# Output stage of a hybrid decoder on one core: the 32 sample rows projected in four column groups beside the first prompt tile, instead of as a ninth tile

## What is computed

```
hn  = (h - mean(h)) * rsqrt(var(h) + EPS)            # per head, 4 heads of 512
out = (hn * gamma + skip * ca) * silu(z)             # 2048 columns
y   = rmsnorm(h_residual + out @ w_out, final_norm_g)   # w_out: 2048 x 1024
```

## Time and profile before

| | us |
|---|---|
| median of 3 runs | 2202.44 |
| lowest and highest | 2199.47, 2211.96 |
| the profiled execution | 2200.57 |
| its span in the profile | 2198.9 |
| mean granted TensorE clock in it | 0.951 of full speed |

### The profile page before, as it was taken

One profiled execution on the slowest core, in us unless ns is written; L12 is line 12 of the kernel. 1 busy time (PEld: TensorE's weight loads), 2 busy tenths in 40 slices (PEclk: granted clock), 3 DMA queues, 4 the chain that ended last, 5 costly groups with the idle time before them and its releaser, 6 DMA issues. The chain is left out here.

```text
span 2198.9 us, 28433 instructions
## 1 busy us (share of the span) xinstructions
PE 1993.0 (91%) x11425; PEld 1640.9 (75%) x11425; DVE 1121.7 (51%) x1819; ACT 674.9 (31%) x1187; POOL 118.4 (5%) x195
## 2 busy tenths in 40 slices
PE   5999998787777989999999899899999999988998
PEld 4999997555434869999999685595586578557885
DVE  5232113888433435534434557756846865785442
ACT  4111112777322314322222422321232232233221
POOL 0000000000221000000000001101100110100000
PEclk7999998999897989999999999999999999989999
DMA  4111112200676224764693425624552653767541
GB/s 155 39 42 55 54 40 93 64 1 1 218 235 208 80 47 93 119 156 119 157 207 117 167 77 191 196 79 161 186 177 91 210 164 115 207 236 226 184 139 34
DMA packets 174647, 282.67 MB, mean 129 GB/s; under 512 B 15683, under 2 KB 110727, under 8 KB 173402
## 3 DMA queue, kind: packets, MB, share of 16 engines
q1 hardware_dynamic: 146533, 179.54, 29.0%
q0 software_dynamic: 27840, 100.80, 13.9%
q10 hardware_dynamic: 144, 0.52, 0.1%
HBM read 185.70 MB, written 95.31 MB: 128 GB/s over the span
## 5 line engine op out<-in xcount | busy, mean ns | idle before, releaser
L1445 PE MATMUL pre_ps<-x_xh,pre_wh 128*128 128x358 f32 (+1 forms) x792 | 261.1, 330 | 6.7 <-DVE pre_wl L1567 6.7
L1446 PE MATMUL pre_ps<-norm_xl,pre_wh 128*128 128x358 f32 (+1 forms) x792 | 259.5, 328 | 0.0
L1447 PE MATMUL pre_ps<-x_xh,pre_wl 128*128 128x358 f32 (+1 forms) x792 | 258.7, 327 | 0.0
L426 PE MATMUL proj_ps<-x_xe,proj_wh 128*128 128x368 f32 x480 | 161.4, 336 | 4.8 <-DVE proj_wl L539 4.8
L428 PE MATMUL proj_ps<-x_xe,proj_wl 128*128 128x368 f32 x480 | 159.9, 333 | 0.0
L427 PE MATMUL proj_ps<-lo_xl,proj_wh 128*128 128x368 f32 x480 | 159.4, 332 | 0.0
L1445 PEld LDWEIGHTS pre_ps<-x_xh,pre_wh 128*128 128x128 f32 x792 | 150.3, 190 | 8.2 <-DVE pre_wl L1567 7.2
L1447 PEld LDWEIGHTS pre_ps<-x_xh,pre_wl 128*128 128x128 f32 x792 | 150.4, 190 | 0.0
L1446 PEld LDWEIGHTS pre_ps<-norm_xl,pre_wh 128*128 128x128 f32 x792 | 150.4, 190 | 0.0
L539 DVE TENSOR_TENSOR proj_wl<-all_w,proj_wh 128x1024 fp32r<-128x1024 f32 x24 | 29.2, 1225 | 194.1 <-ACT proj_wh L501 194.1
L1911 PE MATMUL head_ps<-head_cl,head_wh 128*128 128x358 f32 (+1 forms) x384 | 125.2, 326 | 0.0
(11 more groups left out here) (429 smaller groups left out, 4252.6 us busy)
## 6 DMA issues: line engine op xcount, KB each, us to landing
head_Cs<-in_state_C POOLq DMA_DIRECT2D x20, 1024.0 KB, 9.0
out_C_s<-head_Cs POOLq DMA_DIRECT2D x19, 1024.0 KB, 5.1
x_xnT<-in_cache_sb_k SPq DMA_DIRECT2D x64, 256.0 KB, 3.2
all_w<-in_w_in_c SPq DMA_DIRECT2D x32, 512.0 KB, 9.0
all_w<-in_w_in_a SPq DMA_DIRECT2D x24, 512.0 KB, 3.8
paged_vp<-in_cache_sb_v POOLq DMA_DIRECT2D x48, 256.0 KB, 4.2
head_Cs_top<-in_state_C POOLq DMA_DIRECT2D x12, 1024.0 KB, 9.0
out_C_s<-head_Cs_top POOLq DMA_DIRECT2D x12, 1024.0 KB, 4.7
```

What stands on the lines that cost most here:

```text
L426: pe.matmul(out, wh[:, t % 2, k, :], xh[:, k, c0:c1], start=(k == 0), stop=False)
L1445: pe.matmul(out, wh[:, t % 2, k, :], xh[:, k, c0:c1], start=(k == 0), stop=False)
L1446: pe.matmul(out, wh[:, t % 2, k, :], xl[:, k, c0:c1], start=False, stop=False)
L1447: last = pe.matmul(out, wl[:, t % 2, k, :], xh[:, k, c0:c1], start=False, stop=(k == KD - 1))
```

## The change

The sample rows lose their place as the last tile. They are prepared right after tile 0 (order of tiles in `turned`: 0, 8, 1, ..., 7; `place(i)` is a tile's position in it) with `a_s` and `b_s` of their own, and their projection is made inside `project_first`:

- Ten **rounds** of four full-float32 products each, in the manner of `sample_parts`: 32 output partitions each, at partitions 0, 32, 64, 96. A round covers two chunks and both halves: groups 0 and 1 take the first chunk, 2 and 3 the second, and the halves alternate between banks 6 and 7. Chunks 4 to 15 use the loaded weights ("raw", six rounds), chunks 0 to 3, whose raw weights are gone, the high and the low part (four rounds).
- The raw round of a pair is issued before the odd chunk ahead of it (`sample_raw(4)` before chunk 3, ..., `sample_raw(14)` before chunk 13). `low_weights(k)` for `k >= 4` now waits until the raw round has read the pair.
- ACT copies banks 6 and 7 to `parts`; after the first half of tile 1 two `fold` products sum the four groups.
- On SP two loads of 256 KB (`a_s`, `b_s`, 128 bytes a piece) and the sample rows' `num` (256 KB) are issued ahead of the six pairs. The loads of tile 1 wait for the transposes of the samples. Residual rows are loaded one tile later.
- The last tile stored is now a prompt tile of 128 rows.

```diff
+        def place(i):
+            return turned.index(i)
@@ sync
             load_rows(0)
+            sp.wait_ge(cs_out[0], 16 * CS_USES[0] * HC)
+            load_sample_gates()
             heads_stored(sp)
+            sp.dma_start(num[1][0:NS, :], num_dram[NT, 0:NS]).then_inc(num_in[1], 16)
             for j in range((KI - WA_K) // 2):
                 k = slice(WA_K + 2 * j, WA_K + 2 * j + 2)
                 sp.dma_start(wo_b[:, 2 * j:2 * j + 2, :], src_w[:, k, :]).then_inc(wo_in[j], 16)
                 if j == 3:
                     load(1)
-            load_rows(1)
+            load_rows(NT)
             sp.dma_start(g[:, :], d["final_norm_g"]...).then_inc(g_in, 16)
-            for i in range(2, NT + 1):
+            for i in range(2, NT):
                 load(i)
-                load_rows(i)
+                load_rows(i - 1)
+            load_rows(NT - 1)
@@ load(i)
+                sp.wait_ge(t_full, HC * (2 if i == 1 else place(i - 2) + 1))
@@ tensor
+            rounds = [("raw", k) for k in (4, 6, 8)] + [("high", 0), ("low", 0), ("raw", 10), ("high", 2), ("low", 2), ("raw", 12), ("raw", 14)]
+
+            def sample_groups(kind, k):
+                n, right = rounds.index((kind, k)), {"raw": wo_at, "high": woh_at, "low": wol_at}[kind]
+                for x in range(4):
+                    half, kk = (x + n) % 2, k + x // 2
+                    row = right(kk)[:, BANK * half:BANK * (half + 1)]
+                    last = pe.matmul(ps[NS * x:NS * (x + 1), 6 + half, :], a_s[:, kk, :], row if kind == "raw" else row.bitcast(F32),
+                                     start=(n < 2), stop=(n >= len(rounds) - 2))
+                return last
+
+            def sample_raw(k):
+                pe.wait_ge(wo_in[(k - WA_K) // 2], 16)
+                if k == WA_K:
+                    pe.wait_ge(o_done, 2 * HC)
+                sample_groups("raw", k).then_inc(raw_used, 1)
+
+            def fold():
+                pe.wait_ge(h_done, 2)
+                for half in range(2):
+                    pe.wait_ge(parts_done, half + 1)
+                    pe.matmul(ps[0:NS, 4 + half, :], const[:, C_FOLD:C_FOLD + NS], parts[:, half, :], start=True, stop=True).then_inc(fold_full, 1)
+
             def project_first():
                 for k in range(KI):
+                    if k == 2:
+                        turn(NT)
+                    elif k >= 3 and k % 2 == 1 and k + 1 < KI:
+                        sample_raw(k + 1)
+                    if k == 8:
+                        sample_groups("high", 0)
+                        sample_groups("low", 0)
+                    elif k == 10:
+                        sample_groups("high", 2)
+                        sample_groups("low", 2)
...
-            for i in range(1, NT + 1):
+            for i in range(1, NT):
                 project(i, 0)
-                if i < NT:
+                if i == 1:
+                    fold()
+                if i + 1 < NT:
                     turn(i + 1)
                 project(i, 1)
@@ scalar
             high_output(0, 1)
+            normalise(NT)
             high_weights(4)
             high_output(0, 2)
             high_weights(5)
             high_output(0, 3)
             for k in range(6, KI):
                 high_weights(k)
+            normalise(1)
+            copy_parts()
+            for e in range(HC):
+                high_output(1, e)
+            squares(0)
+            root(0)
@@ vector
             low_output(0, 1)
-            low_weights(4)
             gate(0, 3)
             low_output(0, 2)
-            low_weights(5)
+            for e in range(HC):
+                gate(NT, e)
             low_output(0, 3)
-            for k in range(6, KI):
+            for k in range(4, KI):
                 low_weights(k)
             outputs(1)
...
+                if i == 1:
+                    add_samples()
                 add(i, 0)
+                if i == 1:
+                    finish(NT)
@@ low_weights(k)
+                if k >= WA_K:
+                    dve.wait_ge(raw_used, (k - WA_K) // 2 + 1)
```

More of the change, by code:

```diff
@@ L2502, in odd_output @@
         stat = s.sb("stat", [P, 2, 2])
+        a_s, b_s = s.sb("a_s", [P, KI, NS]), s.sb("b_s", [P, KI, NS])
+        assert s.place["b_s"] == s.place["a_s"] + 4 * KI * NS
+        parts = s.over("a_s", "parts", [P, 2, BANK], F32)
         wo_a, wol_a, woh_a = ahead[3:]
@@ L2531, in rows_at, with slot, nums_in @@
             return (P, seq(i)) if i < NT else (NS, slice(0, NS))
+        def place(i):
+            return turned.index(i)
+        def slot(i):
+            return 1 if i == NT else i % 2
+        def nums_in(i):
+            return 16 * (1 if i == NT else i // 2 + 1 + i % 2)
         def woh_at(k):
@@ L2606, in project @@
                         pe.wait_ge(ol_done, HC * i + k // KH + 1)
-                    high, low = oh[i % 2][:, k, 0:rows], ol[i % 2][:, k, 0:rows]
+                    high, low = oh[i % 2][:, k, :], ol[i % 2][:, k, :]
                     pe.matmul(out, high, woh_at(k)[:, c], start=(k == 0), stop=False)
@@ L2648, in high_output @@
                 k = slice(KH * e, KH * (e + 1))
-                act.wait_ge(o_done, HC * i + e + 1)
+                act.wait_ge(o_done, HC * place(i) + e + 1)
                 act.activation(oh[i % 2][:, k, 0:rows], a[i % 2][:, k, 0:rows], ACT.Copy).then_inc(oh_done, 1)
@@ L2660, in squares, with copy_parts @@
                 rows, _ = rows_at(i)
-                act.wait_ge(h_done, 2 * i + 2)
-                act.activation(sq[0:rows, :], h[0:rows, i % 2, :], ACT.Square, accum_out=stat[0:rows, i % 2, 0:1]).then_inc(ss_done, 1)
+                j = place(i) % 2
+                if i == NT:
+                    act.wait_ge(hs_done, 2)
+                else:
+                    act.wait_ge(h_done, 2 * i + 2)
+                act.activation(sq[0:rows, :], h[0:rows, j, :], ACT.Square, accum_out=stat[0:rows, j, 0:1]).then_inc(ss_done, 1)
             def root(i):
                 rows, _ = rows_at(i)
-                act.wait_ge(msq_done, i + 1)
-                act.activation(stat[0:rows, i % 2, 0:1], stat[0:rows, i % 2, 1:2], ACT.Sqrt).then_inc(rms_done, 1)
+                j = place(i) % 2
+                act.wait_ge(msq_done, place(i) + 1)
+                act.activation(stat[0:rows, j, 0:1], stat[0:rows, j, 1:2], ACT.Sqrt).then_inc(rms_done, 1)
+            def copy_parts():
+                act.wait_ge(raw_used, (KI - WA_K) // 2)
+                for half in range(2):
+                    act.activation(parts[:, half, :], ps[:, 6 + half, :], ACT.Copy).then_inc(parts_done, 1)
             normalise(0)
@@ L2690, in gate @@
             def gate(i, e):
-                j, (rows, _) = i % 2, rows_at(i)
+                j, m, (rows, _) = i % 2, place(i), rows_at(i)
                 k = slice(KH * e, KH * (e + 1))
-                o = a[j][:, k, 0:rows]
+                o, shift = (a_s[:, k, :], b_s[:, k, :]) if i == NT else (a[j][:, k, :], bv[j][:, k, :])
                 src = ps[:, e, :].rearrange("p (k r) -> p k r", r=P)[:, :, 0:rows]
-                if e == 0:
+                if e == 0 and i == NT:
+                    dve.wait_ge(as_in, 16)
+                    dve.wait_ge(bs_in, 16)
+                elif e == 0:
                     dve.wait_ge(a_in[j], 16 * (i // 2 + 1))
                     dve.wait_ge(b_in[j], 16 * (i // 2 + 1))
-                dve.wait_ge(t_full, HC * i + e + 1)
+                dve.wait_ge(t_full, HC * m + e + 1)
                 dve.tensor_tensor(o, src, o, ALU.mult).then_inc(t_done, 1)
-                dve.wait_ge(t_done, HC * i + e + 1)
-                dve.tensor_tensor(o, o, bv[j][:, k, 0:rows], ALU.add).then_inc(o_done, 1)
+                dve.wait_ge(t_done, HC * m + e + 1)
+                dve.tensor_tensor(o, o, shift, ALU.add).then_inc(o_done, 1)
             def low_output(i, e):
```

90 lines of the change are left out of this document (55 added, 35 removed).

## The result

| us | before | after |
|---|---|---|
| median (11 runs each) | 2205.39 | 2194.74 |
| lowest, highest | 2197.66, 2211.96 | 2185.36, 2197.43 |
| profiled execution, span | 2200.57, 2198.9 | 2197.43, 2195.7 |
| output stage in it | 237.5 | 226.4 |

The ratio is 0.9942 with a 95% interval of 0.9923 to 0.9961: 0.58% faster, 0.39 to 0.77%. I had put the likeliest case at 0.45%, just inside "within 0.5%"; the measured value lies just outside, on the faster side, and the interval covers both.

What follows compares the result with a forecast made beforehand. TensorE was taken to bound the output stage, except tile 0, which waits 5.78 us for weights. Terms -22.14 - 1.2 + 0.7 + 10.8 + 2.0 sum to -9.8 us, giving 2191.5 us, range 2185.5 to 2200.

Steps and rivals of the forecast that it cites:

- first round to the end of tile 0: Tile 0 from 1978.3 to 2011.1: chunks 3 to 15 18.0 us, transposes 1.7, rounds 11.4, clock 1.5, `low_weights` 0.2.
- tiles 1 to 7 with fold: After tile 0: two adjacent fold products in tile 1 add 2.0 us; removing the samples' 16 transposes in tile 7 saves 1.2.
- tail: End of the run: tile 7's norm and store replace the samples'; only the larger store differs, +0.7 us.
- The stall before the first round: Tile 0, before chunk 3: sample gates wait behind the first weight pair, 4.3 us later; round at 1978.3, TensorE idle 4.5 us.
- The rounds: Tile 0: 1.2 us for a round alone, 2.1 for two adjacent; ten rounds add 11.4 us.
- The clock: Tile 0, after the idle time: 3 us at half clock lose 1.5 us.
- A: Before the first round: first pair only 2 us later, idle about 2, clock full, rounds 1.0; total -15.0 us; chance 0.37.
- B: Tile 0: low parts lag 0.3 us per pair, dearer rounds, or SP queue clogs; total -7 to 0 us; chance 0.13.
- C: Rounds in tile 0: groups do not overlap, a round costs 3.5 us; total +13.8 us, 2215; chance 0.06.
- The chances: Whole kernel: faster by over 0.5% 0.37, within 0.5% 0.56, slower 0.07.

Runs made afterwards that it cites:

- again: The changed kernel itself, unaltered, run and profiled a second time: output stage 225.3 us, ratio 0.9938 to the kernel before.
- run with one product: Changed kernel, from the third round on only the first of a round's four products issued: output stage 226.4 us.
- one without groups: Changed kernel, the same 40 products all written to partitions 0 to 31 of their bank, copy and fold on 32 partitions: output stage 252.5 us.
- gates first and paired rounds: Changed kernel, sample gates ahead of `low_output(0, 2)` and the ten rounds in six places instead of eight: output stage 221.9 us, ratio 0.9935 to before.
- Packed, at the end: Kernel before, samples still the ninth tile, their 96 products made 16 column-group rounds, one copy and two folds: output stage 230.9 us, ratio 0.9979.
- four more rounds: Changed kernel plus four extra rounds in the first tile, two before chunk 6 and two before chunk 12: output stage 230.4 us.
- without one small load: Changed kernel with the load of `b_s` left out and `a_s` added in its place: output stage 223.4 us.
- the gates first: Changed kernel, sample gates ahead of `low_output(0, 2)`: output stage 222.9 us, ratio 0.9940 to before; with rounds also paired, 221.9 us.

## Why the prediction came out as it did

The predicted 2191.5 lies 3.2 below the measured median of 2194.74, inside the range; the sum was -9.8 us, the medians' difference -10.65, the stage's -11.1. That the median came out above 2191.5 although the gain was larger than the sum has nothing to do with the change: the kernel before had 2202.44 in the 3 runs I started from and 2205.39 in 11. Term by term, in the stage's own time:

| term | forecast | measured |
|---|---|---|
| first round, us into the stage | 16.9 | 15.7 (again: 16.1) |
| idle before it | 4.5 | 2.4 (again: 1.1) |
| first pair of weights landed, us into the stage | 12.3 | 10.9 |
| first round to the end of tile 0 | 32.8 | 32.8 (again: 31.3) |
| fifth pair landed, us into the stage | 32.1 | 32.2 |
| tiles 1 to 7 with fold, against 167.8 | +0.8 | +0.5 |
| tail | +0.7 | +0.7 |
| stage | -9.8 | -11.1 (again: -12.2) |

**The stall before the first round** was right in place, chain and releaser, and mis-sized. I took the start as the landing of the first pair (1973.7) plus 4.6 us. In fact the samples' `num` and their normalising, which I had called hidden, stood on the path: ACT came to the pair 0.3 us after it had landed. Put on the old time axis (7.88 us less) the pair landed at 1972.3 and the rounding of chunk 4 began at 1972.6, not at 1973.7. So the three small loads had delayed the first pair by 2.9 us and not by the 4.3 I had added, while the chain behind it took 4.5 of the 4.6 forecast. Why 2.9, when the fifth pair did come 4.4 us later than before, no run here separates. And TensorE was not done with chunk 2 at 1973.8 but at 1974.8 on that axis: the samples' transposes with their switches and a wait for ACT took 1.5 us. The idle time shrank from both ends.

**The rounds** were sized right: 1.20 alone, 0.88 behind another. The run with one product shows that the four overlap wholly, and the one without groups that they would cost 3.46. The Trainium skill gives 3.07x for four packed row tiles (TensorE: Matmul & The Clock Gate, Measured speedup vs the span model). That figure does not carry over to these column groups: 3.46 / 0.88 = 3.9, and the 2.7 us that it would have added to the sum did not come. The 0.3 us between a round by itself and one behind another are 0.09 at the step into the round (0.32 instead of 0.23), 0.12 more to the next ordinary product (1.00) than to a next round (0.88), and 0.11 at the step after that (0.34 instead of 0.23). The Trainium skill's rule that a change of tiling mode drains TensorE (TensorEngine Tiling (Array Packing), Key Properties) fits them, but they do not prove it: the transposes of tile 1, which take no groups, are entered at the ordinary 0.23 and yet followed by a step of 0.31. So most of the last part comes without a change of shape as well.

```profile
2013.06 0.40 PE L2682 MATMUL post_ps<-post_woh_b,post_ol 128*128 128x512 f32 x1
2013.29 1.91 PE L2618 MATMUL post_ps<-all_const,post_num 128*128 128x128 f32 x16
2014.96 0.48 PE L2680 MATMUL post_ps<-post_woh_b,post_oh 128*128 128x512 f32 x1
2015.27 0.39 PE L2681 MATMUL post_ps<-post_wol_b,post_oh 128*128 128x512 f32 x1
```

**The clock** was put at 1.5 us after the idle time. In the first execution the half clock lasted 3.4 us, all of it on the path, which loses 1.7; in the second it fell on work that had slack. The 1.1 us between the two is the size of what cannot be forecast here.

**The rivals.** A (no stall worth the name) is not what happened, but its total of -15 is what the experiment with the gates first and paired rounds reaches (-15.6), by removing the stall; an earlier landing alone (2.9 us later than before, nearer to A's 2 than to my 4.3) did not do it. B lost its ground: `low_weights` made TensorE wait 0.1 us at a few chunks, not 0.3 for each pair, and the transfers bound nothing. C was the right price for something that doesn't happen. **The chances** failed most: with a sum of 0.45% and terms known to a microsecond or two, I gave 0.56 to "within 0.5%" and 0.37 to more; the measured 0.58% is on the other side of a line that lay within the error of the sum, and the honest split was about even.

## What to carry to other kernels

Work moved into a stretch that waits for transfers is paid only beyond that wait, but what it needs first (its loads, its normalising, its gates) stands in the same in-order queues as the work it is moved beside. Here one line of VectorE's order, the sample gates behind an instruction that waits for ScalarE, cost 2.5 to 3.6 us of the gain. Look also at the form that the data has in the new place: here the unsplit weights, which spare six rounds, gave more than the filled wait. Full-float32 products with 32 output partitions cost the same alone as in four groups, so what counts is the number of rounds and of switches between the two kinds. And when a change is small against the drift of an untouched stage, measure the stage that it touches.

## What the runs showed of the hardware

- The stage of the heads, the same instructions each time, took 736.6 to 749.4 us in six executions, with the granted clock between 0.97 and 0.95: a drift of 13 us that has nothing to do with the kernels compared and is larger than the change. That the clock is its cause is only argued from these rows.
- Four full-float32 products of 32 partitions each, with different stationary and moving operands and alternating between two PSUM banks, take 0.88 us together; one takes as long; in one and the same group they take 3.46.
- A column group's price is not tied to one bank: four products in one bank took 0.99 us to the next product, two and two in two banks 1.00.
- The clock fell 2.8 us after the products stopped (1982.6 to 1985.4), after TensorE had already begun again, and rose 3.4 us later. The delay is not the same each time: about 2.1 us in the kernel before, 5.0 us in "Packed, at the end" (1992.7 to 1997.7, after a wait of 4.62 us). With an idle time of 2.4 us before the first round the half clock followed in four executions of four (the first, four more rounds, one product a round, the groups one by one). After 1.1 us (without one small load) or none (the gates first, twice) it did not.
